# Gated output products of the SSM and attention branches: two passes of 1024 columns in place of four iterations of 512

## The reference, cut to what matters

```python
u = rms_norm(h, mix_norm_pre)
proj = u @ w_in        # -> c_q, c_kv, k_r, z, xbc, dt_raw, g_attn, g_ssm
attn = mla_branch(c_q, c_kv, k_r, ...)      # (256, 2048)
ssm = mamba2_branch(z, xbc, dt_raw, ...)    # (256, 4096)
mixed = jax.nn.sigmoid(g_attn) * (attn @ w_attn_o) + jax.nn.sigmoid(g_ssm) * (ssm @ w_ssm_o)
h = h + rms_norm(mixed @ w_out, mix_norm_post)
# then a SwiGLU block (w_gate, w_up, w_down) and a gated per-layer embedding
```

## Time and profile before

| | us |
|---|---|
| median of three runs | 2030.86 |
| the profiled execution, its own time | 2030.8 |
| its span, first to last instruction | 2029.1 |
| TensorE matmul busy | 2017.1 (99%) |
| VectorE busy | 1400.4 (69%) |
| ScalarE busy | 1088.9 (54%) |
| iteration 1 of `so` on TensorE | 619.49 to 684.86 |
| iteration 2 of `ao` on TensorE | 1018.39 to 1062.81 |

### The profile page before, as it was taken

How to read it: one execution, slowest core, us unless ns; L and a number is a source line. 1 busy time by engine, 2 the same in 40 slices (tenths; PEclk the granted TensorE clock), 3 DMA queues, 4 the chain that set the end, 5 groups by cost and what they waited for, 6 DMA issues and landing times.

```text
span 2029.1 us, 31396 instructions
## 1 busy us (share of the span) xinstructions
PE 2017.1 (99%) x10937; PEld 1735.0 (86%) x10937; DVE 1400.4 (69%) x2019; ACT 1088.9 (54%) x1395; POOL 15.4 (1%) x31
## 2 busy tenths in 40 slices
PE   9999999999999999999999999999999999999998
PEld 8888888888888888998888888888888888888886
DVE  7788988888864454675555566666666567878776
ACT  6666666666554444565444465445444445545564
POOL 0000000000000000000000000000000000000000
PEclk9999999999999999999999999999999999999999
DMA  8666666566565555545556756566656656655654
GB/s 237 190 202 193 193 194 197 173 194 195 174 200 188 193 195 186 142 129 166 188 192 212 253 162 225 184 188 195 191 184 193 189 184 227 205 196 203 228 209 144
DMA packets 321378, 390.18 MB, mean 192 GB/s; under 512 B 25928, under 2 KB 248640, under 8 KB 319392
## 3 DMA queue, kind: packets, MB, share of 16 engines
q1 hardware_dynamic: 317920, 369.86, 57.6%
q0 software_dynamic: 3216, 19.24, 2.6%
q10 hardware_dynamic: 176, 0.20, 0.0%
HBM read 384.99 MB, written 4.26 MB: 192 GB/s over the span
## 4 chain that ended last, share of the span: by engine, by line
PE 99%; DVE 1%; DMA 0%; ACT 0%; issue 0%; DVEq 0%; SPq 0%; ACTq 0%
PE acc L555 16%; PE acc L568 15%; PE acc L772 12%; PE acc L774 12%; PE acc L773 12%; PE acc L573 8%; PE acc L557 8%; PE acc L1150 1%; PE acc L1149 1%; PE acc L1151 1%; PE acc L938 1%; PE acc L706 1%; PE acc L531 1%; PE acc L532 1%; PE acc L533 1%; PE acc L869 1%
## 5 line engine op out<-in xcount | busy, mean ns | idle before, releaser
L1754 DVE TENSOR_TENSOR wlo<-raw,whi 128x1024 fp32r<-128x1024 f32 (+1 forms) x671 | 808.1, 1212 | 426.8 <-ACT whi L1234 424.6
L1234 ACT ACTIVATE whi<-raw 128x1024 fp32r<-128x1024 f32 (+1 forms) x672 | 699.4, 1048 | 549.7 <-PE acc L774 288.6
L555 PE MATMUL acc<-u,whi 128*128 128x512 f32 x1408 | 488.7, 394 | 0.0
L557 PE MATMUL acc<-u,wlo 128*128 128x256 f32 x1408 | 390.1, 277 | 0.0
L568 PE MATMUL acc<-u,whi 128*128 128x512 f32 x1376 | 328.6, 391 | 0.0
L555 PEld LDWEIGHTS acc<-u,whi 128*128 128x128 f32 x1408 | 264.0, 187 | 61.3 <-issue 0.2
L568 PEld LDWEIGHTS acc<-u,whi 128*128 128x128 f32 x1376 | 252.8, 188 | 48.7
L772 PE MATMUL acc<-whi,g 128*128 128x512 f32 x720 | 280.5, 390 | 0.0
L773 PE MATMUL acc<-wlo,g 128*128 128x512 f32 x720 | 280.2, 389 | 0.0
L774 PE MATMUL acc<-whi,g 128*128 128x512 f32 x720 | 280.2, 389 | 0.0
L557 PEld LDWEIGHTS acc<-u,wlo 128*128 128x128 f32 x1408 | 264.4, 188 | 0.0
(11 more groups left out here) (392 smaller groups left out, 1942.0 us busy)
## 6 DMA issues: line engine op xcount, KB each, us to landing
raw<-w_in_in SPq DMA_DIRECT2D x208, 512.0 KB, 3.7
raw<-w_gate_in SPq DMA_DIRECT2D x88, 512.0 KB, 4.1
raw<-w_up_in SPq DMA_DIRECT2D x88, 512.0 KB, 4.4
raw<-w_down_in SPq DMA_DIRECT2D x88, 512.0 KB, 3.8
raw<-w_ssm_o_in SPq DMA_DIRECT2D x64, 512.0 KB, 4.0
raw<-w_in_in SPq DMA_DIRECT2D x64, 256.0 KB, 4.0
raw<-w_attn_o_in SPq DMA_DIRECT2D x32, 512.0 KB, 4.2
raw<-w_out_in SPq DMA_DIRECT2D x32, 512.0 KB, 4.5
```

The costliest lines, as they stand in the source:

```text
L555: T.matmul(bank(b), wh[:, j, i * P:i * P + P], src[:, kt, :, :].rearrange("p a s -> p (a s)"), start=start and j == 0, stop=False, skip_gr ...
L557: last = T.matmul(bank(b)[:, 0:SEQ], wl[:, j, i * P:i * P + P], src[:, kt, 0, :], start=False, stop=stop and j == len(kts) - 1, skip_group ...
L1234: S.activation(whi[:, slot, 0:w], raw[:, slot, 0:w], ACT.Copy).then_inc(sem("hi_ready"), 1)
L1754: V.tensor_tensor(wlo[:, slot, 0:w], raw[:, slot, 0:w], whi[:, slot, 0:w].bitcast(F32), ALU.subtract) \
```

## The change: what it does

`so` becomes two passes of 48 chunks, `ao` two passes of 32, with chunks of one tile by 1024 columns (`wide_chunk`, the former `plain_chunk` of `dn`, made general). The gate product (chunks 0 to 15) fills banks 0 to 3, the branch product banks 4 to 7. Loops and helpers of the seven-product scheme take the phase as an argument, and their lists for `so` and `ao` are empty. Both passes of `so` are written out on ScalarE, VectorE and TensorE. In the core of the diff:

```diff
-    "so": (24, 4),
+    "so": (48, 2),
-    "ao": (16, 4),
+    "ao": (32, 2),
+SEVEN = {"so": (), "ao": (), "dn": (1, 2, 3, 4, 5, 6, 7, 8)}
...
+        def wide_chunk(phase, it, c, first_bank, src, kt, start, stop):
+            begin(phase, it, c)
+            wh, wl = ring(c, 512)
+            order = [(half, blk) for half in range(2) for blk in range(2)]
...
+            for half, blk in order:
...
+                if phase == "ao" and it == 0 and c == 0 and (half, blk) == (0, 1):
+                    pe.wait_ge(sem("v_ev"), 8)
+                last = one_tile(first_bank + 2 * half + blk, src, kt, blk, wh, wl, half, start, stop)
+            last.then_inc(sem("chunk_done"), 1)
```

TensorE, `so`:

```diff
+        for it in range(2):
+            for c_ in range(16):
+                wide_chunk("so", it, c_, 0, u, c_, c_ == 0, c_ == 15)
+                if it == 0 and c_ == 2:
                     norms_qkv()
+                if it == 1 and c_ == 6:
+                    rotary_key()
...
+            for i in range(16):
+                if i == 2:
+                    pe.wait_ge(sem("sg_so"), it + 1)
...
+                wide_products("so", it, i)
```

TensorE, `wo`:

```diff
-                if it == 0 and c_ == 2:
-                    mixed_turned(3)
+                if it == 0 and c_ in (1, 2):
+                    mixed_turned(1 + c_)
```

ScalarE, `so`:

```diff
         def so_gate(it):
-            group_end("so", it, 7)
-            act.wait_ge(sem("so_ev"), it + CREDIT["so_ev"])
-            S.activation(sg[:, :, :], psum[:, 0:2, :], ACT.Sigmoid).then_inc(sem("sg_so"), 1)
+            group_end("so", it, 15)
+            for half in range(2):
+                cols = slice(1024 * it + 512 * half, 1024 * it + 512 * half + 512)
+                last = S.activation(m[:, :, cols], psum[:, 2 * half:2 * half + 2, :], ACT.Sigmoid)
+            last.then_inc(sem("sg_so"), 1)
...
-            if c_ == 10:
+            if c_ == 17:
                 act.wait_ge(sem("ssm_lo"), GROUPS + CREDIT["ssm_lo"])
+                act.wait_ge(sem("rkv_ready"), 1)
                 so_gate(0)
-            if c_ == 14:
+            if c_ == 18:
                 act.wait_ge(sem("angles"), 2)
                 S.activation(sin[:, :], a_s[:, :], ACT.Sin)
                 S.activation(cos[:, :], a_c[:, :], ACT.Sin).then_inc(sem("rope_tab"), 1)
```

VectorE, `so` iteration 0 and then `ao`:

```diff
-            if c_ == 8:
+            if c_ == 14:
                 dve.wait_ge(sem("pos_in"), 32)
...
-            if c_ == 9:
                 angle(a_s[:, :], 0.0)
-            if c_ == 11:
+            if c_ == 15:
...
+        values(8)
+        for it in range(2):
+            for c_ in range(0 if it else 2, 32):
                 split("ao", it, c_)
                 if it == 0 and c_ == 3:
                     attn_max(8)
-                    values(8)
```

VectorE, `wo` iteration 0, after its split of chunk 2:

```diff
+                    ao_evac(2)
                     ao_evac(3)
```

More of the change, by code:

```diff
@@ L835, in _ @@
[L835 to L846, removed]
@@ L847, in _, with rotary_key @@
-        last.then_inc(sem("rt_mm"), 1)
-        with pe.Fori(1, 4) as it:
-            so_iter(it)
+        def rotary_key():
+            pe.wait_ge(sem("so_ev"), 1)
+            pe.wait_ge(sem("rope_tab"), 1)
+            pe.wait_ge(sem("c_lo"), 8)
+            T.matmul(bank(4)[:, 0:SEQ], rotk, kr[0:64, :], start=True, stop=True)
+            T.matmul(bank(4)[:, SEQ:2 * SEQ], dupk, kr[0:64, :], start=True, stop=True).then_inc(sem("krot_mm"), 1)
+            pe.wait_ge(sem("rkv_ready"), 1)
+            for i, r in enumerate((r_kv, r_q)):
+                for blk in range(2):
+                    o = i * SEQ + blk * P
+                    last = T.transpose(bank(5)[:, o:o + P], r[:, blk * P:blk * P + P], ident)
+            last.then_inc(sem("rt_mm"), 1)
@@ L976, in mixed_turned @@
                     o = j % 2 * SEQ + blk * P
-                    last = T.transpose(bank(4 + j // 2)[:, o:o + P], prod[:, blk, j * P:j * P + P], ident)
+                    last = T.transpose(bank(4 + n % 2 * 2 + j // 2)[:, o:o + P],
+                                       m[:, blk, 512 * n + j * P:512 * n + j * P + P], ident)
             last.then_inc(sem("mt_mm"), 1)
[L980 to L987, removed]
+        pe.wait_ge(sem("rope_t"), 15)
+        pe.wait_ge(sem("rot_cp"), 8)
+        pe.wait_ge(sem("kn_ev"), 8)
+        pe.wait_ge(sem("q_ev"), 8)
+        for it in range(2):
+            for c_ in range(16):
+                wide_chunk("ao", it, c_, 0, u, c_, c_ == 0, c_ == 15)
                 if it == 0 and c_ == 1:
@@ L991, in ao_iter @@
                     attn_turn(8)
[L992 to L1001, removed]
                 if it == 0 and c_ == 9:
                     attn_values(8)
-        for it in range(4):
[L1006 to L1012, removed]
+                if it and c_ in (3, 5):
+                    mixed_turned((c_ - 3) // 2)
+            if it == 0:
+                pe.wait_ge(sem("o_lo"), 8)
+            else:
+                pe.wait_ge(sem("ao_lo"), 2)
+            for i in range(8):
+                if i == 1:
+                    pe.wait_ge(sem("sg_ao"), it + 1)
+                wide_products("ao", it, i)
+        for it in range(4):
             if it > 1:
@@ L1093, in _ @@
             ff_iter(it)
[L1096 to L1107, removed]
-                last = one_tile(c_bank(it, half, blk), g, dn_tile(c), blk, wh, wl, half, c == 0, stop)
-            last.then_inc(sem("chunk_done"), 1)
         def last_plain_chunks():
@@ L1433, in _ @@
                 S.activation(cos[:, :], a_c[:, :], ACT.Sin).then_inc(sem("rope_tab"), 1)
-        with act.Fori(1, 4) as it:
-            for c_ in range(24):
-                split("so", it, c_)
-                if c_ == 10:
-                    so_gate(it)
+        for c_ in range(48):
+            split("so", 1, c_)
+            if c_ == 17:
+                so_gate(1)
         def weights_turned(n):
@@ L1772, in newton, with wide_low @@
+        def wide_low(phase, it, c):
+            if not is_seven(phase, c):
+                split(phase, it, c)
+            elif c % 2 == 0:
+                seven_sums(phase, it, c)
         def newton(ms, r0, tmp, final, dst=None, scale=1.0):
@@ L2219, in _ @@
             if c_ == 2:
-                so_evac(3)
+                so_evac(1)
         def attn_iter(it, after):
```

496 lines of the change are left out of this document (261 added, 235 removed).

## The result

The changed kernel takes 2034.08 us (median of 20 runs, 2033.68 to 2035.3) against 2030.89 us for the kernel before (20 runs, 2030.71 to 2031.32). The ratio is 1.0016, interval 1.0010 to 1.0023: 3.2 us or 0.16% longer, inside the 0.2% that the prediction called no change. The forecast was 2033.6 us, in a range of 2030.6 to 2036.3. The profiled execution took 2034.08 us around a span of 2032.2 us.

A forecast was written before the change was run, and what follows sets the result against it. TensorE, busy 99% of the span, was taken to bound the kernel. Exposed waits of 0.9 us (gates of so) and 1.8 us (values(8)) made 2.7 us, added to 2030.86: 2033.6 us, range 2030.6 to 2036.3.

The forecast's parts named there:

- the two places: The gates of so (0.9 us) and values(8) at the start of ao (1.8 us), where TensorE would wait.
- values(8): Chunk 0 of ao: TensorE waits before its fourth matmul for VectorE's copy of the attention values; 1.8 us lost.
- The gate in pass 0: so, pass 0: chunk 18 late by 0.30 us behind two sigmoids, chunk 19 by another 0.29 us behind the sines.
- Rival B: Table loads at so's gates and sines hold ScalarE 1.38 us longer; 6.8 us lost in all, 2037.7 us; chance 0.06.
- The gate in pass 1: so, pass 1: 0.30 us lost before chunk 18, table load included, because the sines replaced the sigmoid's table.
- Everything else: Matmuls, transposes and the other moved steps in so, ao and wo: unchanged or hidden, 0 us.
- `wo` was hidden: wo iteration 0: chunk 7's split shifts 2.4 us against a 4.1 us margin; 0.7 us shows if DMA doubles that.
- A: The waits at values(8) and so's gates are hidden: nothing lost, 2030.9 us; chance 0.11.
- C: The 1.8 us pause in ao drops the clock to 1.2 GHz, costing 3 to 5 us, 2036.5 to 2039; chance 0.02.
- the argument against it in the prediction: After the last matmul the clock stays 1.00 as far as 2025, so idling over twice the pause keeps 2.4 GHz.
- the prediction's sign of being wrong: Anywhere in the trace after: a clock below 1.00 before the end would show the forecast wrong; no size given.
- D's slower side: so's straight code or the wider rows slow TensorE's stream; no size or chance of its own given.

The follow-up runs named there:

- a_waits: Changed kernel with ScalarE's two extra waits in pass 0 of so moved ahead of the split of chunk 17; 2033.47 us, one run.
- a_both: Changed kernel with values(8) earlier, bank 1 last in ao's chunk 0, ScalarE's two waits before chunk 17's split, sines behind chunk 22; 2031.43 us.
- b_ kernels: Follow-up kernels made from the kernel before, each with an edit.
- b_unroll: Kernel before with its hardware loops over so written out as straight code on TensorE, ScalarE and VectorE; 2030.98 us.
- a_turns: a_both with the four groups of transposes of mixed merged into two of 16; 2031.44 us.
- b_values: Kernel before, with values(8) ahead of VectorE's splits of ao and TensorE waiting for it before chunk 0's fourth matmul; 2032.84 us.
- b_shift: Kernel before with its tiles from CONST0 on placed 2048 bytes further on; 2030.81 us.
- a_gate16: Changed kernel with both gates of so one chunk earlier, behind ScalarE's split of chunk 16 instead of 17; 2039.83 us.

## Why the prediction was right, and where not

**The mechanism held.** TensorE pays only where a margin ends, and the two places were the ones forecast. The number of TensorE's instructions, the distance of starts away from the two places and the clock did not change; `wo` has no wait.

**`values(8)`: 1.8 forecast, 1.94 measured.** VectorE's order was read rightly. Its timeline in the changed kernel:

```profile
924.07 1.22 DVE L1786 TENSOR_TENSOR wlo<-raw,whi 128x1024 fp32r<-128x1024 f32 x1
925.21 0.69 DVE L2260 TENSOR_TENSOR g<-acc,g 128x512 fp32r<-128x512 f32 x1
925.81 0.42 DVE L2288 TENSOR_TENSOR rt<-qs,sin 128x256 f32<-128x256 f32 x1
926.26 0.42 DVE L2292 TENSOR_TENSOR qr<-rt 128x256 f32<-128x256 f32 x1
926.60 0.68 DVE L2275 TENSOR_TENSOR vt_last<-acc,r_tok 128x512 f32<-128x512 f32 x1
```

It starts at 926.60, which is the 925.78 of the earlier trace rows and the 0.82 by which all is late here; the pause is 1.81 us. The 0.11 us that a restarted TensorE loses between its first two matmuls was missing from the sum.

**The gate in pass 0: 0.59 forecast, 0.63 measured.** The branch product starts at s = 596.19, and the splits were forecast at s + 3.37 and s + 6.38; the split of chunk 18 stands at 599.57, s + 3.38, and the next at 602.58, s + 6.39. Chunk 18 was late by 0.32 us (forecast 0.30); chunk 19 started at 604.93 (forecast s + 8.75 = 604.94), but it was needed later than forecast, by the 0.11 us of the restart and by 0.06 of slightly wider distances behind it (up to 0.24 for 0.23), so that 0.09 was left and not 0.29. With two restarts of 0.11 the sum comes out near the forecast, partly by luck; the whole step, with the wider distances, is 0.74. The drain of about 1.38 us that the Trainium skill, "ScalarE: Activation LUTs", section "What ACT_TABLE_LOAD costs", states isn't there: the sigmoid starts 0.02 us after its load ends, as in the earlier trace rows. Rival B is out.

**The gate in pass 1: 0.30 forecast, 0 measured.** This is the step that failed. The prediction charged pass 1 with a load behind the wait, as in pass 0, "because the sines have replaced the sigmoid's table". The load is there (725.06), but 4.3 us ahead of the sigmoid, under the wait for TensorE. In these traces the load goes ahead of a wait that the activation itself carries, and not ahead of a wait instruction of its own; a_waits shows the same in pass 0 by changing the place of two waits alone. Counted from the start of the branch product (729.17 here, 596.19 in pass 0), the sigmoids start 1.36 us sooner than in pass 0, and so does all behind them: 0.32 us too late becomes 1.04 us in time.

**Everything else: 0 forecast, some 0.6 us measured.** The prediction put all the rest at nothing, and a_both shows 0.6 us with no wait. TensorE's stream through the changed stages is not where it lies: in the trace of a_both the nth matmul is late by 0.18 us where `so` starts and by 0.14 in `wo`, and that much is there already 18 us into the span, ahead of all that the change touches. (At that point the traces of the changed kernel and its variants are late by 0.02 to 0.33 us and those of the b_ kernels by 0.08 to 0.20, so it may be no more than the spread of single traces.) Another 0.1 us lies behind the last matmul: from its start to the end of the span it is 9.00 us before, and 9.1 in every trace of the changed kernel and its variants, but in b_unroll too. The rest lies outside the span. Device time less span is 1.88 us on average in a_both and in a_turns, and 1.66 us in b_values, b_unroll and b_shift and 1.67 in the runs of the kernel before. So 0.2 us lie there, and they come with the changed kernel's code or transfers, neither with the wait, nor with straight code for `so`, nor with the layout. Which part does it remains open. The rows of 4 KB in `so` and `ao` and the queue of their loads were not tried alone; nor is it clear why the first matmul starts at 1.36 us on the span's axis in the changed kernel and at 2.01 before (by the 22nd matmul the two are within 0.07 us). Single traces are no help below 0.2 us: b_unroll's last matmul is 0.29 us late in its trace, with a median of 0.1.

The loss of 3.2 us is thus 1.9 for `values(8)`, 0.7 to 0.8 for the gate in pass 0 and 0.6 for what is open. That the forecast of 2.7 came near is in part luck: its term of 0.3 for pass 1 was not there, and it stood in for part of the 0.6 that no term covered.

**`wo` was hidden, about as forecast.** The split of chunk 7 in the changed kernel, on ScalarE and then on VectorE:

```profile
1125.51 1.06 ACT L1255 ACTIVATE whi<-raw 128x1024 fp32r<-128x1024 f32 x1 [5.16 <-DMA raw<-w_out_in]
1126.60 1.23 DVE L1786 TENSOR_TENSOR wlo<-raw,whi 128x1024 fp32r<-128x1024 f32 x1 [4.78 <-ACT whi L1255]
```

Both are 3.77 us later than in the earlier trace rows, and TensorE is 2.72 us later there. Its chunk 7 starts at 1129.87, the split ends at 1127.83 and is usable some 0.06 later: 2.0 us are left, where the prediction had 4.1 less 2.4, so 1.7. The DMA did not double the shift.

**Rivals.** A is out: both waits show. C is out for this change: the clock behind the pause of 1.65 us is 1.00, in this window from 927.30 on:

```profile
927.30:935.00 7.70, 7.66 (x43) 6.13 (x44) 2.50 (x6) 1.24 (x3) 0.00 (x0) 1.00 0.59 189
```

But its mechanism is real here: a_gate16 shows it behind a pause of 2.87 us. And the argument against it in the prediction does not hold. The window of the earlier trace rows ends at 2025.00, and the next two of the same trace show the clock falling while TensorE is idle:

```profile
2025.00:2026.00 1.00, 0.00 (x0) 0.00 (x0) 1.00 (x3) 0.00 (x0) 0.00 (x0) 0.90 0.65 240
2026.00:2029.00 3.00, 0.00 (x0) 0.00 (x0) 0.49 (x1) 0.00 (x0) 0.00 (x0) 0.50 0.73 270
```

So the clock fell some 5.3 us after the end of the last matmul, and in the trace of b_values it did so only 2.5 us after it: the granted clock is 1.00 from 2022.60 to 2025.10 and 0.50 behind. In the changed kernel, too, it falls only behind the last matmul, at 2026.8, so the prediction's sign of being wrong (a clock below 1.00 before the end) is met by the idle end of every trace and says nothing. That the pause of 1.8 us left the clock alone is measured; how long a pause would be safe is not shown. D's slower side (straight code or wider rows) is small: b_unroll gives 0.1 us for the straight code, a_both 0.6 us for everything but the waits, and TensorE's stream in `so` and `ao` shows no loss.

## What to carry to other kernels

When work is regrouped without changing it, list for every helper engine how many prepared chunks cover its detour, and price only the places where that cover ends: two such places, read to 0.1 or 0.2 us from the timelines, made most of this result. A PSUM bank that is reused earlier than before can turn a copy that nobody waited for into a wait. Two repairs are to move that wait behind the matmuls of other banks and to move the copy up in its engine's order; together they took all of the 1.9 us back. Put those plain waits of ScalarE that are long fulfilled ahead of the work before, and let the activation carry the last wait, so that its table load passes under it. Before you argue from an idle stretch that the clock holds, look at the whole stretch. None of the repairs beat the kernel before: the repaired version is level with it within the interval (1.0004) and 0.6 us above it by the medians, so the wider chunks themselves brought nothing.

## What the runs showed of the hardware

- A TensorE that waited restarts slowly: its first matmul is 0.50 us long instead of 0.39 and the next starts 0.34 us after it instead of 0.23, whether the delay was 0.1 us (604.93) or 1.8 us (927.34).
- In a_gate16 a pause of 2.87 us in `so` was followed, about 1.1 us after the restart, by some 3 us at 1.2 GHz; pauses of 1.65 us (changed kernel), 1.66 us (b_values) and 1.52 us (pass 1 of a_gate16) were not. The clock also fell with TensorE idle at the end, 5.3 us after the end of the last matmul in the kernel before and 2.5 us after it in b_values.
- A table load of 1.28 us went ahead of a wait carried by its activation (load at 725.06, sigmoid at 729.37), and stayed behind wait instructions of their own (load at 596.45, sigmoid at 597.75).
- A wait shown in brackets counts from the modelled end of the instruction before it. For a 128 x 512 matmul it is 0.16 us less than the time lost: 0.16 against 0.32, and 1.65 against 1.81.
